# Second sparse attention: scores right behind the root, output blocks beside its softmax, output gates in twos

## The reference

```
x = first_block(...)
u = rms_norm_2(x, norm1_g) @ w_in            # split into the inputs of all three mixers
y_a = dsa_mixer(...)                         # top-k sparse attention, 16 heads of 64
y_b = nsa_mixer(q, kc, vc, ks, vs, kw, vw, gates, ...)   # 16 heads of 64, 2 groups
y_c = ssd_mixer(...)
gates = sigmoid(mg)
mix = gates[0] * (y_a @ w_br_dsa) + gates[1] * (y_b @ w_br_nsa) + gates[2] * (y_c @ w_br_ssd)
x = x + mix @ w_out; x = x + square(relu(norm(x) @ w_ff1)) @ w_ff2

# in nsa_mixer, for a block of 128 queries
s = einsum(q, k_cmp) * scale; s = where(vis, s, NEG)     # 31 compressed keys
p_cmp = softmax(s) * vis
o_cmp = einsum(p_cmp, v_cmp)
imp = einsum(p_cmp, cover)                               # chooses 4 blocks of 64 keys
```

## Time and profile before

| | us |
|---|---|
| median of 3 runs | 2971.26 (2971.16 to 2973.33) |
| profiled execution, own time | 2973.71 |
| its span | 2971.9 |
| PE busy | 2771.3 (93%) |
| DVE busy | 1631.5 (55%) |
| ACT busy | 1135.3 (38%) |
| mean granted PE clock | 0.96 of full |

### The profile page before, as it was taken

How to read it: one execution, slowest core, us unless ns; L and a number is a source line. 1 busy time by engine, 2 the same in 40 slices (tenths; PEclk the granted TensorE clock), 3 DMA queues, 4 the chain that set the end, 5 groups by cost and what they waited for, 6 DMA issues and landing times.

```text
span 2971.9 us, 38479 instructions
## 1 busy us (share of the span) xinstructions
PE 2771.3 (93%) x13807; PEld 2227.5 (75%) x13807; DVE 1631.5 (55%) x2981; ACT 1135.3 (38%) x1860; POOL 73.3 (2%) x84
## 2 busy tenths in 40 slices
PE   7999999989999999998988997989899988999998
PEld 5567888878888788887765885667677777778887
DVE  5335726446554662634866337753677766464452
ACT  4343322225553422222437324852355543232221
POOL 0000000000000000000000000000011110000000
PEclk9999999979999999997999988999899998999999
DMA  3112333212111233232120220002222222323331
GB/s 136 42 57 71 114 94 97 99 36 79 56 56 36 85 108 98 93 99 71 57 71 1 83 81 29 1 22 92 72 70 71 64 67 69 121 92 100 95 102 64
DMA packets 60079, 219.33 MB, mean 74 GB/s; under 512 B 6448, under 2 KB 6576, under 8 KB 59824
## 3 DMA queue, kind: packets, MB, share of 16 engines
q1 hardware_dynamic: 58352, 211.33, 22.5%
q0 software_dynamic: 1600, 6.29, 0.6%
HBM read 213.41 MB, written 4.19 MB: 73 GB/s over the span
## 4 chain that ended last, share of the span: by engine, by line
PE 79%; DVE 10%; ACT 5%; issue 3%; DVEq 3%; ACTq 0%; DMA 0%; POOL 0%; SPq 0%
PE ps L366 22%; PE ps L368 22%; PE ps L367 22%; PE ps L447 1%; PE ps L500 1%; DVE big L2965 1%; PE ps L1788 1%; DVE ring_lo L306 1%; DVEq L3018 1%; PE ps L751 1%; PE ps L1331 1%; PE ps L455 1%; DVE work L1862 1%; ACT ring_hi L299 1%; PE ps L1769 1%
## 5 line engine op out<-in xcount | busy, mean ns | idle before, releaser
L366 PE MATMUL ps<-a_hi,ring_hi 128*128 128x512 f32 x1960 | 790.6, 403 | 57.0 <-DVE ring_lo L306 30.8
L368 PE MATMUL ps<-a_hi,ring_lo 128*128 128x512 f32 x1960 | 776.1, 396 | 0.0
L306 DVE TENSOR_TENSOR ring_lo<-ring,ring_hi 128x1024 fp32r<-128x1024 f32 x381 | 466.1, 1225 | 555.0 <-ACT ring_hi L299 523.8
L367 PE MATMUL ps<-a_lo,ring_hi 128*128 128x512 f32 x1896 | 750.5, 396 | 0.0
L299 ACT ACTIVATE ring_hi<-ring 128x1024 fp32r<-128x1024 f32 x381 | 400.7, 1055 | 526.1 <-PE ps L368 524.0
L366 PEld LDWEIGHTS ps<-a_hi,ring_hi 128*128 128x128 f32 x1960 | 376.4, 192 | 141.9 <-issue 28.1
L368 PEld LDWEIGHTS ps<-a_hi,ring_lo 128*128 128x128 f32 x1960 | 375.9, 192 | 81.3
L367 PEld LDWEIGHTS ps<-a_lo,ring_hi 128*128 128x128 f32 x1896 | 364.3, 192 | 75.1 <-issue 1.2
L367 PE MATMUL ps<-hid_lo,ring_hi 128*128 128x512 f32 x960 | 375.5, 391 | 0.0
L366 PE MATMUL ps<-hid_hi,ring_hi 128*128 128x512 f32 x896 | 349.7, 390 | 5.6 <-DVEq L1067 5.6
L368 PE MATMUL ps<-hid_hi,ring_lo 128*128 128x512 f32 x896 | 349.2, 390 | 0.0
(11 more groups left out here) (395 smaller groups left out, 3240.8 us busy)
## 6 DMA issues: line engine op xcount, KB each, us to landing
ring<-weights SPq DMA_DIRECT2D x395, 512.0 KB, 3.5
h<-x SPq DMA_DIRECT2D x1, 2048.0 KB, 10.0
residual<-h POOLq DMA_DIRECT2D x2, 1024.0 KB, 4.8
h<-residual POOLq DMA_DIRECT2D x1, 2048.0 KB, 11.2
out<-h POOLq DMA_DIRECT2D x1, 2048.0 KB, 7.6
tab<-tables SPq DMA_DIRECT2D x1, 1648.0 KB, 16.1
big<-positions SPq DMA_DIRECT2D x1, 256.0 KB, 3.4
col<-columns SPq DMA_DIRECT2D x1, 164.5 KB, 4.2
```

Of the source, the lines that this page charges most:

```text
L306: dve.tensor_tensor(lo, M.ring[:, b % RING, :], hi.bitcast(F32), ALU.subtract).then_inc(M.sem("blocks_split"), 1)
L366: pe.matmul(out, w_hi, hi, start=start, stop=False)
L367: pe.matmul(out, w_hi, lo, start=False, stop=False)
L368: return pe.matmul(out, w_lo, hi, start=False, stop=stop)
```

## The change

In the first sparse attention the wait for the root and the reciprocal leave round 40 of the top-k and go behind its last round and the rest of block 20. PE's spreads go four behind t = 20 and five behind t = 21. In the second, PE does all eleven spreads and the scores right behind `first_branch(1)`, and the blocks 2 to 7 stand behind the scores, between the turns. DVE's order follows: `first_branch(1)` behind the last scaling, 2 to 5 between the four `weigh`, 6 behind the comparisons, 7 between the masks of the two groups. The product with the visible keys is made on the 16 inverse sums of a quarter instead of on its 512 columns. The rests 8 and 9 go behind the pair attention. The blocks of `nsa_out` are laid out, and worked through, as two gates and then two y blocks.

```diff
-def branch_out_pe(pe, M, name, y_hi, y_lo, per_tile, unroll, wait_y):
+def branch_out_pe(pe, M, name, y_hi, y_lo, wait_y):
+    with pe.Fori(0, NT // 2) as i:
+        for n in range(4):
+            u, out = n % 2, n // 2
+            if not out:
+                pe.wait_ge(M.sem(f"{name}_free"), i * 2 + (u + 1))
+            b = FIRST[name] + n
+            wait_split(pe, M, b, i, 4)
+            if out:
+                wait_y()
...
+def branch_out_act(act, M, name):
+    with act.Fori(0, NT // 2) as i:
+        for u in range(2):
+            act.wait_ge(M.sem(f"{name}_free"), i * 2 + (u + 1))
+            act.wait_ge(M.sem("blocks_used"), i * 4 + (FIRST[name] + u + 1))
+            act.activation(M.sq[:, u, :], M.bank(2 * u), ACT.Sigmoid).then_inc(M.sem("gates_ready"), 1)
+            round_block(act, M, FIRST[name] + u + 2, i, 4)
+        for u in range(2):
+            round_block(act, M, FIRST[name] + u + 4, i, 4)
...
     dve.drain().then_inc(M.sem(f"{name}_free"), 2)
     before()
+    with dve.Fori(0, NT // 2) as i:
+        for u in range(2):
+            rest_block(dve, M, FIRST[name] + u + 2, i, 4)
+        for u in range(2):
+            dve.wait_ge(M.sem("gates_ready"), i * 2 + (u + 1 + NT * BRANCHES.index(name)))
+            dve.wait_ge(M.sem("blocks_used"), i * 4 + (FIRST[name] + 2 + u + 1))
+            m = tile_at(M.m, i * 2 + u)
+            dve.tensor_tensor(M.ssum[:, :], M.bank(2 * u + 1), M.sq[:, u, :], ALU.mult)
+            dve.drain()
+            dve.tensor_tensor(m, m, M.ssum[:, :], ALU.add)
             dve.drain().then_inc(M.sem(f"{name}_free"), 1)
+            rest_block(dve, M, FIRST[name] + u + 4, i, 4)
... dsa_pe
-        if t == 18:
-            spread(0)
-            spread(1)
         if t == 20:
-            for k in range(2, 5):
+            for k in range(4):
                 spread(k)
-    for k in range(5, 9):
+    for k in range(4, 9):
         spread(k)
... dsa_dve
-            if n == 40:
-                dve.wait_ge(M.sem("norm_root"), 1 + M.past("dsa_norm", "root"))
-                dve.reciprocal(M.inv[:, 0:72], M.root[:, 0:72]).then_inc(M.sem("norm_inverse"), 1)
...
     rest(12)
-    scaled(0)
-    scaled(1)
+    dve.wait_ge(M.sem("norm_root"), 1 + M.past("dsa_norm", "root"))
+    dve.reciprocal(M.inv[:, 0:72], M.root[:, 0:72]).then_inc(M.sem("norm_inverse"), 1)
     rest(13)
-    for k in range(2, 5):
+    for k in range(4):
         scaled(k)
     rest(14)
-    for k in range(5, 9):
+    for k in range(4, 9):
         scaled(k)
     rest(15)
... nsa_pe
     first_branch(1)
-    for k in range(4):
-        spread(k)
-    first_branch(2)
-    for k in range(4, 8):
-        spread(k)
-    first_branch(3)
-    for k in range(8, 11):
+    for k in range(11):
         spread(k)
...
-    for u in range(4, NT):
-        first_branch(u)
-        if u >= 5:
-            turned(u - 5)
+    first_branch(2)
+    first_branch(3)
+    turned(0)
+    first_branch(4)
+    turned(1)
+    turned(2)
+    first_branch(5)
     turned(3)
+    first_branch(6)
+    first_branch(7)
... nsa_act
-    for n in range(17, 21):
-        rounded(n)
-    exp(0)
-    exp(1)
+    rounded(17)
+    rounded(18)
+    for n in range(4):
+        exp(n)
+    rounded(19)
+    rounded(20)
+    keep(0)
     rounded(21)
-    exp(2)
-    exp(3)
+    keep(1)
+    keep(2)
     rounded(22)
-    keep(0)
+    keep(3)
     rounded(23)
-    keep(1)
     rounded(24)
-    keep(2)
-    keep(3)
... nsa_dve
     first_branch(0)
-    for k in range(4):
+    for k in range(7):
         scaled(k)
     rest(3)
+    for k in range(7, 11):
+        scaled(k)
+    dve.drain()
     first_branch(1)
-    for k in range(4, 8):
-        scaled(k)
-    rest(4)
-    first_branch(2)
-    for k in range(8, 11):
-        scaled(k)
-    dve.drain()
-    rest(5)
-    first_branch(3)
...
+        dve.tensor_tensor(heads(R.top), heads(R.top), M.t("cmp_seen", P)[:, 0:P:32].unsqueeze(1).broadcast_to([P, 4, QT]),
+                          ALU.mult)
+        dve.drain()
         dve.tensor_tensor(rows16(p), rows16(p), wide(R.top), ALU.mult)
-        dve.drain()
-        dve.tensor_tensor(heads(p), heads(p), four(M.t("cmp_seen", P)), ALU.mult)
         dve.drain()
...
+    rest(4)
+    first_branch(2)
+    weigh(0)
+    rest(5)
+    first_branch(3)
+    weigh(1)
+    weigh(2)
     rest(6)
     first_branch(4)
-    weigh(0)
+    weigh(3)
     rest(7)
-    weigh(1)
     first_branch(5)
-    weigh(2)
-    weigh(3)
-    rest(8)
-    first_branch(6)
...
-    rest(9)
-    first_branch(7)
+    first_branch(6)
...
+        if g == 0:
+            first_branch(7)
...
     R.pairs.dve(dve, M, gate)
-    branch_out_dve(dve, M, "nsa_out", 1, 2, lambda: split_y_dve(dve, M, "nsa", R.y))
+    rest(8)
+    rest(9)
+    branch_out_dve(dve, M, "nsa_out", lambda: split_y_dve(dve, M, "nsa", R.y))
```

More of the change, by code:

```diff
@@ L1898 @@
 BRANCHES = ["nsa_out", "ssd_out"]
-def branch_out_pe(pe, M, name, y_hi, y_lo, per_tile, unroll, wait_y):
[L1902 to L1908, removed]
+def branch_out_pe(pe, M, name, y_hi, y_lo, wait_y):
+    used = M.sem("blocks_used")
+    with pe.Fori(0, NT // 2) as i:
[7 more added lines that the diff above has]
+                wait_y()
+            hi, lo = (y_hi, y_lo) if out else (M.a_hi, M.a2_lo)
@@ L1909, in branch_out_pe @@
             for k in range(BLK):
-                mm = split_matmul(pe, M, M.bank(2 * (u % 2)), b, k, M.a_hi[:, k, :], M.a2_lo[:, k, :], k == 0, k == 7)
+                mm = split_matmul(pe, M, M.bank(2 * u + out), b, k, hi[:, k, :], lo[:, k, :], k == 0, k == 7)
             mm.then_inc(used, 1)
[L1912 to L1919, removed]
@@ L1922, in branch_out_act @@
[L1922 to L1929, removed]
@@ L1932, in branch_out_dve @@
-def branch_out_dve(dve, M, name, per_tile, unroll, before, first=False, last=False):
+def branch_out_act(act, M, name):
[7 more added lines that the diff above has]
+            round_block(act, M, FIRST[name] + u + 4, i, 4)
@@ L1935, in branch_out_dve @@
+def branch_out_dve(dve, M, name, before):
     dve.drain().then_inc(M.sem(f"{name}_free"), 2)
     before()
[L1937 to L1948, removed]
-                dve.drain()
-                dve.tensor_tensor(m, m, M.ssum[:, :], ALU.add)
+    with dve.Fori(0, NT // 2) as i:
[8 more added lines that the diff above has]
+            dve.tensor_tensor(m, m, M.ssum[:, :], ALU.add)
@@ L1951, in branch_out_dve @@
             dve.drain().then_inc(M.sem(f"{name}_free"), 1)
-            rest_block(dve, M, FIRST[name] + u * (1 + per_tile) + per_tile + 2, i, unroll * (1 + per_tile))
-            if last:
-                split_dve(dve, m, tile_at(M.in_hi, t), tile_at(M.in_lo, t)).then_inc(M.sem("mix_split"), 1)
+            rest_block(dve, M, FIRST[name] + u + 4, i, 4)
 def split_y_dve(dve, M, name, y):
@@ L1964, in branch_of_pairs_pe @@
 def branch_of_pairs_pe(pe, M, name, before):
-    branch_out_pe(pe, M, f"{name}_out", M.hid_hi[:, 0:NT, :], M.hid_hi[:, NT:2 * NT, :], 1, 2,
-                  lambda blk: pe.wait_ge(M.sem("y_split"), before + NT))
+    branch_out_pe(pe, M, f"{name}_out", M.hid_hi[:, 0:NT, :], M.hid_hi[:, NT:2 * NT, :],
+                  lambda: pe.wait_ge(M.sem("y_split"), before + NT))
 TOPK_RESTS = (7, 12, 17, 21, 25, 28, 32, 35, 38, 41, 43, 46)
@@ L2426, in keep @@
         act.activation(R.pt[:, QUARTERS[n], :], M.bank(4 + n), ACT.Copy).then_inc(M.sem("nsa_cmp_kept"), 1)
-    for n in range(17, 21):
-        rounded(n)
-    exp(0)
-    exp(1)
+    rounded(17)
[5 more added lines that the diff above has]
+    keep(0)
     rounded(21)
-    exp(2)
-    exp(3)
+    keep(1)
+    keep(2)
     rounded(22)
-    keep(0)
+    keep(3)
     rounded(23)
-    keep(1)
     rounded(24)
-    keep(2)
-    keep(3)
     R.pairs.act(act, M)
-    branch_out_act(act, M, "nsa_out", 1, 2)
+    branch_out_act(act, M, "nsa_out")
 def nsa_dve(dve, M, R, dsa):
@@ L2502, in nsa_dve @@
     first_branch(0)
-    for k in range(4):
+    for k in range(7):
         scaled(k)
     rest(3)
-    first_branch(1)
-    for k in range(4, 8):
-        scaled(k)
-    rest(4)
-    first_branch(2)
-    for k in range(8, 11):
+    for k in range(7, 11):
         scaled(k)
     dve.drain()
-    rest(5)
-    first_branch(3)
+    first_branch(1)
     rows16 = lambda x: x.rearrange("p (g n) -> p g n", n=32)
@@ L3407, in lay_weights @@
     w_nsa = v["w_br_nsa_2"][0].reshape(2, 8, 64, D).transpose(1, 0, 2, 3).reshape(D, D)
-    put("nsa_out", branch(1, w_nsa))
+    twos = branch(1, w_nsa).reshape(NT // 2, 2, 2, BLK, P, P).transpose(0, 2, 1, 3, 4, 5)
+    put("nsa_out", twos.reshape(-1, P, P))
     z, sx = w["sz"], w["sx"]
```

## The result

| | before | after |
|---|---|---|
| median, us | 2971.21 (2969.38 to 2973.33, 4 runs) | 2946.02 (2942.95 to 2947.74, 4 runs) |
| profiled execution: span / own time | 2971.9 / 2973.71 | 2946.0 / 2947.74 |
| PE busy / mean granted clock | 2771.3 / 0.96 | 2761.0 / 0.965 |

The ratio is 0.9912, 95% interval [0.9898, 0.9927]: the medians differ by 25.2 us, and the interval reaches from 21.7 to 30.3. The forecast of 20.7 us lies outside it.

A forecast was written before the change was run, and what follows sets the result against it. PE carries 79% of the chain of waits, so only places where it idles or is outlasted can be won. 8.8 + 6.4 + 5.5 = 20.7 off 2971.26 gives 2950.6 us; 8 in 10 range 2946 to 2956.5.

The forecast's parts named there:

- A: First attention's top-k stage: without DVE's wait for the root, PE never waits there; gains 8.8 us.
- C: Second attention's output stage: PE's 5.56 us hole before y shrinks to 1.7 behind two gates; gains 5.5 us.
- B: Second attention, spreads and scores up to the pairs: scores start 10.4 us earlier; gains 6.4 us.
- Rivals 3 and 4: 3: a hole stays in A or C, 2956 to 2960 us, chance 0.09; 4: B gains nothing, 2957.0, chance 0.04.
- 2: Rival in the second attention: eleven spreads count as light work and lower PE's clock; 2955.3 us; chance 0.12.
- 5: Rival in the second attention: PE's clock falls in the spreads and doesn't come back; slower, 2977 us; chance 0.03.

The follow-up runs named there:

- e7: The kernel before with ten idle matmuls added on PE ahead of block t = 21 of the first attention; 2969.22 us, ratio 0.9995.
- e12: The kernel before with five idle matmuls added on PE ahead of block t = 21 of the first attention; 2966.70 us, ratio 0.9990.
- e1: The kernel before with only a blank line added; 2968.95 us, ratio 0.9996.
- e11: The changed kernel with the product with the visible keys made on all 512 columns again; 2946.36 us, ratio 0.9914 to the kernel before.
- e4: The kernel before with only the second attention's output blocks changed to two gates, then two y blocks; 2964.58 us, ratio 0.9985.
- e8: The changed kernel with turns 2 and 3 of the second attention each one block later; 2941.54 us, ratio 0.9902 to the kernel before.

## Why the prediction was too small

**What held.** A: forecast 8.8, measured 8.95, and 8.9 alone; the mechanism as well, with the outputs 5.44 apart. C: forecast 5.5, measured 5.50 in its stage; the hole is 1.47 where 1.7 was said. In B the scores start 10.54 us earlier, counted from the reciprocal (28.22 us behind it before, 17.68 after), against 10.4; PE's hole before turn 2 is 3.56 against 3.9, turn 2 is slow (1.11) as said, DVE waits for rest 7; the spreads run at full rate (32 in 1.97 us). Rivals 3 and 4 didn't come about. Nor did 2: the clock fell in the scores, behind the spreads, as it did in the earlier trace rows (2.6 us into them by those rows, as 0.78 over 4.70 us says, and not the 3.5 that I wrote). Nor did 5.

**The step that failed** is the sum: "All three stages follow one another, so gains add." It takes every untouched stage as it was. S2 and S3 weren't, by -2.17 and -3.14, because A moved them by 9 us and PE's half-rate stretches didn't move with them. e7 and e12 show that a shift alone does that, in the kernel before. These 5.3 us are as large as the whole miss (25.9 - 20.7 = 5.2 by the profiled executions, 4.5 by the medians). The other deviations nearly cancel: A +0.15; S4 and S5 together +0.75 (8.37 less 1.22, against 6.4); S7 and the part ahead of the root -1.0. That they cancel is luck.

**B's size.** To the first pair mask I had 6.9; it is 8.37 against the execution that I had, and 6.74 against e1's. The difference is the 1.6 us stretch that lay in S4 in the one and in S3 in the other. It shows in the first rest behind the softmax's first half: it came 48.86 us behind the reciprocal, now 36.67, 12.2 earlier and not 10.4; in e1 it comes at 47.20, and against that it is 10.5 earlier. So in B too what was mis-sized is where the clock was low, not a wait. The wait for rest 7 was 3.72 and not 2.8. The product on 16 columns costs 0.19 us and I had 0.25. I put the whole edit at 1.8 us; by e11 it is worth 0.65 in its stage, as turn 2 and block 5 get less of the clock behind the shorter hole (0.68 against 0.78), and nothing that shows in the total. By the formula of the Trainium skill, VectorE: DVE Perf Modes, section on the TRN2 errata, it is estimated at 0.17 us, and the trace's 0.18 and 0.19 are nearer to that than to the reciprocal's 0.25.

By the Trainium skill, TensorE: Matmul & The Clock Gate, section on HAM oscillation, groups of matmuls with waits between can lose the clock each time. The trace agrees for block 5 behind turn 2 (0.68 of full over the two), though e11 shows that the same group with a longer wait can keep more of it (0.78). It doesn't cover S3, where PE never waits (busy 96.59 of 96.59 us in before) and the stretch follows a group of small matmuls. By the same page of the Trainium skill, in its section on what is actually happening, the window over which activity is watched runs free of the program, so the point at which the clock changes depends on where in it the first matmul lands. That would fit the shifts of e7 and e12, though no run here shows the window itself. The trace doesn't agree with a reading by which each execution of one program then differs: these stages repeat to 0.1 us while the root moves by 8.

**What stays open.** That S5 takes 1.2 us more in the change doesn't come from B: it takes 150.23 with B alone, and 151.5 in e7 and e12, which are the kernel before with a pad. Likewise S7 takes 1.4 more in e7 and e12. So a shift alone can do either; at which instructions was not followed up, nor for the 2.0 of S7 in e4. Nor can I say beforehand at which place a stretch falls: the runs show that it depends on place, not by which rule.

## What to carry to other kernels

Where a profile shows stretches of half clock in which PE is busy, a change that shortens something ahead of them can remove or add some of them, so a sum over the touched stages has an uncertainty of about the size of these stretches; here 1.6 us each in full blocks and 2.2 in the pairs, five us in all. Look for them where a group of small matmuls or a wait stands ahead of full ones. Cut both executions at the same events and compare the untouched stages before a difference is put down to an edit, and test a suspicion with a pad of idle matmuls, read in the stages and not in the total. A hole closed on PE can open another at the next consumer (e8), so look where the engine stands next.

## What was not expected of the hardware

- Added work made the kernel no slower: 2.2 us of idle matmuls gave 0.9995 [0.9986, 1.0004] (e7), 1.05 us gave 0.9990 [0.9981, 0.9999] (e12); from the root to the end both took 2.7 us less.
- PE on full blocks of 512 columns, busy for the whole of a window, was granted 0.51 of the clock at 1706.50 in before, behind 3.30 us of small matmuls, and 1.00 at the same work behind the same matmuls in e12.
- The place of a stretch repeats with the distance from the work ahead: six executions agree to 0.1 us in S2 and S3, while their roots lie between 1500.10 and 1508.28 us.
- A hole of 4.07 us was followed by four turns in 0.69 us (e11), one of 3.56 by 1.11, one of 4.27 by 16 scores in 3.68 (full rate: 2.43).
